# A two-layer hybrid model on one core: the first product of each MLP group read from its bank, and new orders in attention, dense head and MLP opening

## The reference

```python
h = layer_norm(x, ln_emb_g, ln_emb_b)
for l in range(2):
    (...) = split_columns(h @ w_in[l])
    y_a = mamba2_ssd(...)                 # state space mixer
    y_b = mla(...)                        # latent attention, 4 heads, causal
    y_c = retention(...)
    y_d = nsa(...)                        # compressed, selected and window attention
    mix = concatenate([y_a, y_b, y_c, y_d]) @ w_out[l]
    h = layer_norm(ALPHA * h + mix, ln1_g[l], ln1_b[l])
    ff = square(relu(h @ w_mlp1[l])) @ w_mlp2[l]      # 1024 -> 4096 -> 1024
    h = layer_norm(ALPHA * h + ff, ln2_g[l], ln2_b[l])
```

## Time and profile before

| | us |
|---|---|
| three runs | 2863.94, 2865.5, 2869.27 |
| median | 2865.5 |
| profiled execution: own time | 2868.43 |
| profiled execution: span | 2866.6 |
| attention, layer 1 and layer 2 (between barriers) | near 280 and 286 |
| dense stage, layer 1 and layer 2 | near 779 and 757 |

### The profile page before, as it was taken

The page is one execution under the profiler, slowest core; times in us unless marked ns, Lnnn a source line. Parts: engine busy times, 40 slices in busy tenths (PEclk is TensorE's granted clock), DMA queues, the critical chain, the costliest instruction groups (busy, mean ns, idle before and its releaser), DMA issues. The chain is left out here.

```text
span 2866.6 us, 37139 instructions
## 1 busy us (share of the span) xinstructions
PE 2732.7 (95%) x13986; PEld 2187.6 (76%) x13986; DVE 1797.8 (63%) x2939; ACT 1136.9 (40%) x1817; POOL 249.7 (9%) x220
## 2 busy tenths in 40 slices
PE   5999989999989999999999999899999899999997
PEld 5899856655867887888889998566568688878886
DVE  5654454454787776786855544625547877758778
ACT  3422223434355554433433222234343555543343
POOL 3221212000000000000012212210000000000000
PEclk9999988999999999999999999889999999999999
DMA  4223233102315445986621233421032254579865
GB/s 168 65 67 102 89 100 73 32 1 81 96 65 174 144 146 197 385 307 241 220 85 59 63 94 96 105 46 30 1 110 89 90 160 144 155 249 369 288 229 189
DMA packets 254360, 387.29 MB, mean 135 GB/s; under 512 B 38608, under 2 KB 126800, under 8 KB 254184
## 3 DMA queue, kind: packets, MB, share of 16 engines
q1 hardware_dynamic: 254184, 384.92, 41.3%
HBM read 288.05 MB, written 96.83 MB: 134 GB/s over the span
## 5 line engine op out<-in xcount | busy, mean ns | idle before, releaser
L2734 ACT ACTIVATE att_PT<-att_ST 128x512 f32<-128x512 f32 (+2 forms) x244 | 135.1, 555 | 337.6 <-PE att_ST L2627 203.2
L1616 PE MATMUL mix_acc<-mix_whi,x_hi 128*128 128x256 f32 (+1 forms) x640 | 185.4, 290 | 0.0
L994 PE MATMUL dense_tr<-mlp_w,mlp_a 128*128 128x512 f32 x448 | 175.3, 391 | 5.6 <-DVE mlp_w L1292 5.6
L1618 PE MATMUL mix_acc<-mix_whi,x_lo 128*128 128x256 f32 (+1 forms) x640 | 180.0, 281 | 0.0
L1617 PE MATMUL mix_acc<-mix_wlo,x_hi 128*128 128x256 f32 (+1 forms) x640 | 179.9, 281 | 0.0
L996 PE MATMUL dense_tr<-mlp_w,mlp_a 128*128 128x512 f32 x448 | 174.4, 389 | 0.0
L995 PE MATMUL dense_tr<-mlp_w,mlp_a 128*128 128x512 f32 x448 | 174.3, 389 | 0.0
L994 PE MATMUL dense_acc<-mlp_w,mlp_a 128*128 128x512 f32 x448 | 174.3, 389 | 0.0
L996 PE MATMUL dense_acc<-mlp_w,mlp_a 128*128 128x512 f32 x448 | 174.3, 389 | 0.0
L995 PE MATMUL dense_acc<-mlp_w,mlp_a 128*128 128x512 f32 x448 | 174.3, 389 | 0.0
L644 POOL TENSOR_TENSOR norm_rstd<-norm_var,norm_power 128x1 f32<-128x1 f32 x32 | 29.8, 931 | 1476.7 <-DVE norm_var L624 1476.7
(11 more groups left out here) (432 smaller groups left out, 7488.9 us busy)
## 6 DMA issues: line engine op xcount, KB each, us to landing
mlp_w_raw<-w_mlp SPq DMA_DIRECT2D x124, 512.0 KB, 5.7
blocks<-h SPq DMA_DIRECT2D x32, 1792.0 KB, 8.2
mlp_a_raw<-blocks SPq DMA_DIRECT2D x72, 512.0 KB, 4.5
mlp_raw<-w_mlp SPq DMA_DIRECT2D x66, 512.0 KB, 6.0
ahead<-w_in SPq DMA_DIRECT2D x20, 1024.0 KB, 6.5
mlp_temp<-blocks SPq DMA_DIRECT2D x38, 512.0 KB, 4.7
residual<-h SPq DMA_DIRECT2D x32, 512.0 KB, 3.8
h<-residual SPq DMA_DIRECT2D x32, 512.0 KB, 9.2
```

Of the source, the lines that this page charges most:

```text
L994: pe.matmul(out, ah, wh, start=(ch == 0 and k == 0), stop=False, skip_group_check=True)
L1616: pe.matmul(out, xh, whi[b][:, k, 0:n], start=(k == 0), stop=False)
L1618: mm = pe.matmul(out, xl, whi[b][:, k, 0:n], start=False, stop=(k == KT - 1))
L2734: act.activation(PT[0:width, n % 3, c0:512], ST[0:width, n % 2, c0:512], ACT.Exp).then_inc(s.exp_ready, 1)
```

## The change

It has five parts.

1. MLP, first part: from group 2 on ACT no longer copies the first product. DVE's `rest1` reads the bank itself, and PE's product (g,7) waits for `rest1` (`f_ready`) in place of the copy. 28 copies are gone.
2. MLP opening: ACT's activations of group 1 come behind its copy of (2,2), and DVE's `rests(1)`, `quarter22(1)`, `quarter11(1)` move from (1,7) to (2,2).
3. Dense head: ACT and DVE begin with the weights' row 0, then alternate tile and row; PE multiplies tile 0 with rows 0 and 1 as soon as tile 0 is split, then tile 1.
4. Attention opening: turns and places of the first four units are woven into the maxima.
5. Attention: the first half of `u` moves three steps ahead (`CMP0 - 4`), the four key copies five steps ahead (`KEYS0 = FIRST_HALF - 5`).

```diff
             turn_y(0)
             turn_y(1)
-            pe.wait_ge(s.y_lo, 4)
-            for k in range(KT):
+            for t in range(2):
+                pe.wait_ge(s.y_lo, 2 * t + 2)
+                for k in range(2):
+                    pe.wait_ge(s.wo_lo, k + 1)
+                    for half in range(2):
+                        products(t, half, k)
+            turn_y(2)
+            for k in range(2, KT):
...
-                if 1 <= k < NT - 1:
+                if k < NT - 1:
                     turn_y(k + 1)
...
-            y_highs(0)
             for k in range(KT):
...
                 act.activation(wo_hi[:, k, :], raw_of(k), ACT.Copy).then_inc(s.wo_hi, 1)
-                if k == 0:
-                    y_highs(1)
+                if k < 2:
+                    y_highs(k)
...
-            y_lows(0)
             for k in range(KT):
                 dve.wait_ge(s.wo_hi, k + 1)
...
-                if k == 0:
-                    y_lows(1)
+                if k < 2:
+                    y_lows(k)
...
                     if i in (4, 3, 7):
-                        pe.wait_ge({4: s.copied2, 3: s.copied5, 7: s.copied1}[i], g + 1)
+                        pe.wait_ge({4: s.copied2, 3: s.copied5, 7: s.copied1 if g < 2 else s.f_ready}[i], g + 1)
...
-                    elif i == 1:
-                        if g >= 2:
-                            act.wait_ge(s.f_ready, g - 1)
+                    elif i == 1 and g < 2:
                         act.activation(copy1[:, g % 2, :], acc[:, 2 + g % 2, :], ACT.Copy).then_inc(s.copied1, 1)
...
                             if g == 2:
+
+                                activate(1, 4)
+                                activate(1, 3)
                                 square(1, 6)
                             square(g - 1, 7)
...
                     elif (g, i) == (1, 7):
                         square(0, 7)
-                        activate(1, 4)
-                        activate(1, 3)
...
                 def rest1(g):
-                    dve.wait_ge(s.copied1, g + 1)
                     dve.wait_ge(s.read21, g + 1)
-                    dve.tensor_tensor(f[:, g % 2, :], f[:, g % 2, :], copy1[:, g % 2, :], PLUS).then_inc(s.f_ready, 1)
+                    if g < 2:
+                        dve.wait_ge(s.copied1, g + 1)
+                        first = copy1[:, g, :]
+                    else:
+
+                        dve.wait_ge(s.multiplied, at[g, 1] + 1)
+                        first = acc[:, 2 + g % 2, :]
+                    dve.tensor_tensor(f[:, g % 2, :], f[:, g % 2, :], first, PLUS).then_inc(s.f_ready, 1)
...
+                        elif (g, i) == (2, 2):
+                            rests(1)
+                            quarter22(1)
+                            quarter11(1)
+                    elif (g, i) == (0, 1):
+                        rests(0)
+                    elif (g, i) == (1, 7):
+                        block_sums(0)
...
+        KEYS0 = FIRST_HALF - 5
...
                     for u_ in first_units:
                         maxima([(u_, at) for at in range(len(pieces[u_]))])
-                    for u_ in first_units:
-                        turn_maxima(u_)
+                        if u_:
+                            turn_maxima(u_ - 1)
+                    turn_maxima(first_units[-1])
...
-                        if FIRST_HALF <= n < FIRST_HALF + 4:
-                            key_highs(1 + (n - FIRST_HALF) // 2, (n - FIRST_HALF) % 2)
+                        if KEYS0 <= n < KEYS0 + 4:
+                            key_highs(1 + (n - KEYS0) // 2, (n - KEYS0) % 2)
...
                     for u_ in first_units:
                         maxima([(u_, at) for at in range(len(pieces[u_]))])
-                    for u_ in first_units:
+                        if u_ >= 2:
+                            place(u_ - 2)
+                    for u_ in first_units[-2:]:
                         place(u_)
...
-                        if n == CMP0 - 1:
+                        if n in (CMP0 - 4, CMP0 - 1):
```

More of the change, by code:

```diff
@@ L1237, in block_sums, with rests @@
                     mm.then_inc(s.blocks_ready, 1)
+                def rests(g):
+                    gather(g)
+                    rest12(g)
+                    rest21(g)
+                    rest1(g)
                 def collect(p):
@@ L1250, in collect @@
                             block_sums(g - 1)
-                    elif (g, i) in ((0, 1), (1, 7)):
-                        if g:
-                            block_sums(0)
-                        gather(g)
-                        rest12(g)
-                        rest21(g)
-                        rest1(g)
-                        if g:
-                            quarter22(g)
+                        elif (g, i) == (2, 2):
[6 more added lines that the diff above has]
+                        block_sums(0)
                     if i == 6 and g != 1:
                         quarter22(g)
-                    elif i == 7:
+                    elif i == 7 and g != 1:
                         quarter11(g)
@@ L2822, in _ @@
                             write(ends[n - 2])
-                        if n == CMP0 - 1:
+                        if n in (CMP0 - 4, CMP0 - 1):
+                            g0 = (CMP0 - 4, CMP0 - 1).index(n)
                             dve.wait_ge(s.kv_loaded, 16)
                             dve.wait_ge(s.pe_copied, 1)
-                            for g0 in range(2):
-                                dve.tensor_tensor(u[:, g0, :, :], kvT[:].rearrange("p (n j) -> p n j", j=CMP_STRIDE),
-                                                  peT[:, g0 * CMP_STRIDE:(g0 + 1) * CMP_STRIDE].unsqueeze(1).to_broadcast([P, NG, CMP_STRIDE]),
-                                                  ALU.add).then_inc(s.placed, 1)
+                            dve.tensor_tensor(u[:, g0, :, :], kvT[:].rearrange("p (n j) -> p n j", j=CMP_STRIDE),
+                                              peT[:, g0 * CMP_STRIDE:(g0 + 1) * CMP_STRIDE].unsqueeze(1).to_broadcast([P, NG, CMP_STRIDE]),
+                                              ALU.add).then_inc(s.placed, 1)
                         if n == FIRST_HALF + 4:
```

## The result

The changed kernel takes 2847.12 us in the median of four runs (2845.19 to 2852.19), against 2865.57 in the median of four before. The ratio of the changed kernel's time to that before is 0.9937, its 95% interval 0.9919 to 0.9954: 18 us less, 13 to 23. The profiled execution took 2845.19, with a span of 2843.4.

The account below looks back on a forecast made before the run. TensorE, busy 95% of the time, was taken as the bound, so gains come from its waits or its clock. Terms −18.5 −7.7 +1.4 −0.2 +1.6 = −23.4 us gave 2845.0 profiled, 2842.1 median; range 2833 to 2857.

Parts of the forecast that it names:

- the likeliest case: Whole kernel: the forecast as worked out, −23.4 us, 2842.1 us for the median, range 2836 to 2850, chance 0.62.
- Keys: Attention: earlier key copies send the queries' load some 10 us earlier, removing PE's 3.0 us waits; −18.5 us with clock.
- I take all: Attention: low clock behind the removed waits becomes full clock, 2.6 and 10.0 us, so −18.5 rather than −5.8.
- First half of u: Attention: moving it three steps earlier delays row maxima, so PE gives back about what it gains; −0.2 us.
- Head: Dense head: PE starts on tile 0 alone, its first 24 matmuls taking 5.4 us; 3.4 and 4.3 us gained, −7.7.
- Attention opening: Attention start: one link saved, but unit 3's pieces start 1.8 us later; +0.7 us per layer, +1.4 in all.
- MLP opening: MLP groups 1 and 2: the 4.9 us wait before (2,4) reappears before (2,7), up to 0.8 longer; +1.6 us.
- Direct read: MLP's other groups: `rest1` reads the bank at no extra cost and PE is not stopped at (g,7); 0 us.
- The change that doesn't do what it says: Attention: something else holds back the queries' load despite earlier key copies; only −4.9 us left, 2860.6 us, chance 0.08.
- both waits of the MLP opening given away: MLP start: load lands earlier or `rest1` of group 2 passes; −14.7 us instead of +1.6, 2825.8 us, chance 0.08.
- The slower one: Steady MLP groups: DVE reaches `rest1` late and PE waits 2.45 us at each (g,7); +45 us, 2910.7, chance 0.04.
- The clock's rival: Attention: the 3.0 us waits go but low-clock stretches stay behind another pause; 12.6 us not gained, 2854.7 us, chance 0.18.

Follow-up runs that it names:

- head: The kernel before with only the dense head's new order: the stage took 101.63 and 101.66 us in the two layers, against a mean of 105.29 with the old order.
- weave: The kernel before with only the attention opening's turns and places woven into the maxima; ratio not to be told from 1.
- MLP parts: The kernel before with only `rest1` reading the bank itself and the MLP opening's new order; ratio 1.0002.
- direct read: The kernel before with only `rest1` reading the first product from the bank, no new order anywhere; ratio 1.0002.
- the keys alone: The kernel before with only the four key copies of the attention five steps earlier; ratio 0.9975.
- the experiment: The changed kernel with SyncE loading group 3's weights ahead of the store of group 0's block sums; median 2840.67 us in five runs, ratio 0.9915.

## Why the prediction was right

The time, 2847.12, lies in the range (2833 to 2857) and in the likeliest case's own (2836 to 2850), 5 us above the forecast of 2842. What those 5 us are isn't shown: one execution of each kernel was traced.

**Against the profiled execution** the sum was −23.4, and the two spans differ by 23.2; but that agreement is partly luck, as the parts show:

| part | forecast | the two traces | means over all traced kernels |
|---|---|---|---|
| attention behind the first product of `u` (keys, clock) | −18.5 | −17.5 | −17.1 |
| attention opening and `u` | +1.2 | −4.5 | about 0 |
| dense head | −7.7 | −6.5 | −7.1 |
| MLP opening | +1.6 | +2.1 | +1.1 |
| groups from (3,3) on | 0 | 0.00 | 0.00 |
| sum | −23.4 | −26.4 | −23 |

The stretches that the change doesn't touch were 3.2 us longer in the changed kernel's execution. The opening's −4.5 is shorter low stretches at its start (20.5 us twice, where 27.3 and 23.9 stood); eight kernels without the weave and six with it have a mean of 49.9 and 49.7 us from the first maxima to the first product of `u`, so it isn't the change. The interval of the measured difference, 13 to 23 us, has the −23 of the last column at its edge.

**Keys.** Right in mechanism and place: wait gone, load at 469.58. The step on the clock ("I take all") is right in the mean. In the ten layers of five kernels that kept the wait (before, head, weave, MLP parts, direct read), A goes from 227.69 to 235.33, mean 231.63; without any pause it is 223.1 every time. So 8.5 per layer, of which 3 are the wait. That the one profiled execution, with 5.5 and 12.1 us in its two layers, came near twice that mean was luck. What failed is a step beside it, "*First half of u*": it priced the move of `u` for itself, at −0.2, and said nothing of POOL. The earlier keys put POOL's cast and product beside `u`; with the keys alone PE waits 1.9 us and in one layer loses the clock again. With both edits no layer of any traced kernel lost it. `u` moved alone was not built, so what it is worth by itself isn't shown.

**Head.** Right: 3.4 and 4.3 were forecast, 3.5 is the mean. The sign of 24 products in 5.4 us failed in layer 1 of the changed kernel (6.5), where the clock came up late.

**Attention opening.** The mechanism is right: the waits of the turns grew by 2.0 us (8.6 for 6.6), and the opening by 0.5 to 0.6 us per layer (14.6 to 15.2), for a forecast of 0.7. The pieces of unit 3 start 7.8 us behind the first maxima where they started 5.9 behind, for a forecast of 1.8 later.

**MLP opening.** Right in what sets the time, not in the place of the wait. The prediction let the 4.9 us reappear before (2,7); in the trace 6.7 stand ahead of (2,3) and 0.9 ahead of (2,7), as its list of signs allowed. The chain that fixes the start of (2,7) is the one it named: `rest1` stood 8.5 us behind the awaited weights before and after (865.82 to 874.37, 857.70 to 866.25), and M grew by 1.0 and 1.2 for a forecast of 0.8 (over the ten layers of five kernels with the old orders and the six of three with the new, by 0.5). In layer 1 PE's waits themselves grew by less than 0.2 us (4.9 and 2.6 before, 6.7 and 0.9 now); the rest of the 1.0 is PE at a lower clock in the window (0.86 for 0.90). That the load hung on the store ahead of it was argued, and the experiment showed it. It also showed that this chain is worth 1.3 us per layer only, because the wait at (2,3), which hangs on ACT's order, then stays.

**Direct read.** Right: 0.00 us from (3,3) on, with a slack of 1.76 us. A read of the bank is not dearer: the groups of DVE by line, in the window 900 to 1110,

```profile
L1214 DVE TENSOR_TENSOR mlp_f<-mlp_f,dense_acc 128x512 f32<-128x512 f32 x11 | 7.6, 688 | 9.0 <-PE dense_acc L980 9.0
```

show 688 ns where 694 stood with both inputs in SBUF. (The prediction's `rest2` is `rest21`, L1200.) The rule of the Trainium skill, "VectorE: DVE Perf Modes", section on the TRN2 errata, that the prediction set against this part is not borne out here.

**Rivals.** The change that doesn't do what it says, and both waits of the MLP opening given away, are refuted by the traces. The slower one was built, and its mechanism costs time as it said. The clock's rival came true in one layer of one kernel, behind a pause that the prediction hadn't seen. A low stretch in mid-attention with no long wait near it is seen in one kernel, that with the head alone, in layer 1 and layer 2 alike: PE waits 0.61 us for DVE ahead of 570.47, and the windows show the lower level, 0.50, from 573.20 to 576.60, and again from 1979.50:

```profile
560.00:573.20 13.20, 12.53 (x61) 1.00 0.01 1
573.20:576.60 3.40, 3.40 (x10) 0.50 0.00 0
1979.50:1982.90 3.40, 3.40 (x10) 0.50 0.00 0
```

Whether the short pause is the cause isn't shown: the kernel before and the changed one have the same pauses there, and no low stretch behind them. So the section on a second failure mode of the Trainium skill, "TensorE: Matmul & The Clock Gate", which the prediction named, is neither borne out nor refuted here.

## What to carry to other kernels

Where an engine has no slack, an edit is priced by the pause that it takes away and by the low clock behind that pause, and the second can be the larger: 3 us of waiting cost 8.5 here, and in the MLP opening 4 us less waiting, left as two short waits, gave 5.1. Before work is moved earlier for a waiting engine, look at what a third engine will then be doing beside the work already there. And a copy that nobody waits for was worth nothing: 28 of them went, and the time did not move.

## What the runs showed of the hardware

DVE and POOL slow each other when `u` runs beside POOL's casts and products of the keys. A half of `u` (128x1024, both inputs in SBUF) takes 1.22 us with POOL idle. In the changed kernel the second half takes 1.57 to 1.66, with the end of a product and then a cast beside it; with the keys alone the halves take 2.05 and 2.30. POOL's cast beside `u` takes 1.92 us where 1.04 stood, and a product that begins while `u` runs 3.25 where 2.39 stood, but the product that was under way when `u` began kept its 2.37. The Trainium skill, "SBUF — State Buffer", section on who interferes with whom, has this rule: a DVE instruction with two SBUF inputs contends with a GpSimd instruction that reads SBUF. The traces agree with it.

The low stretch behind the same wait of 3 us differs from layer to layer and from trace to trace: A spreads over 7.6 us in ten layers. A sum that takes it from one execution has that error in it.
